# Bf16 matmuls on a filled tile around the first transposes, and five small loads asked for later

## The reference, cut to what matters

```python
def token_mixer(xn, pos_offset, conv_state, ret_state, w_in, conv_w, ret_norm, w_out):
    proj = xn @ w_in                       # 1024 x 3584: xc, gB, gC, q, k, v, g
    ...                                    # short convolution, retention with a state per head
    y = jnp.concatenate([a_out, r_out], axis=-1) @ w_out
    return y, new_conv, new_ret

def decoder_layer(x, ...):
    mix, new_conv, new_ret = token_mixer(rmsnorm(x, norm_mix), ...)
    h = x + mix
    h = h + moe(rmsnorm(h, norm_ffn), w_router, b_router, w_up, b_up, w_down, b_down)
    return h, new_conv, new_ret
...
logits = x @ w_router + b_router           # moe: top 4 of 32 experts
h = xb @ w_up[e] + b_up[e]                 # 1024 x 2048 for each of the 32 experts
return act @ w_down[e] + b_down[e]         # 1024 x 1024 for each
```

## Time and profile before

| | us |
|---|---|
| median of three executions | 1089.33 |
| the profiled execution, its own time | 1087.91 |
| its span, first to last instruction | 1086.0 |
| TensorE's matmul records, busy | 1064.4 |
| VectorE busy | 359.0 |
| memory traffic, mean over the span | 397 GB/s |

### The profile page before, as it was taken

How to read it: one execution, slowest core, us unless ns; L and a number is a source line. 1 busy time by engine, 2 the same in 40 slices (tenths; PEclk the granted TensorE clock), 3 DMA queues, 4 the chain that set the end, 5 groups by cost and what they waited for, 6 DMA issues and landing times.

```text
span 1086.0 us, 13145 instructions
## 1 busy us (share of the span) xinstructions
PE 1064.4 (98%) x5670; PEld 447.3 (41%) x5671; DVE 359.0 (33%) x569; ACT 152.6 (14%) x302; POOL 12.1 (1%) x28
## 2 busy tenths in 40 slices
PE   8999999999999999999999999999999999999997
PEld 6888764333333333333333333333333333333332
DVE  3455534322222222222222222222332222222234
ACT  2121144111111001111111111011111111011113
POOL 1000000000000000000000000000000000000002
PEclk9999999999999999999999999999999999999999
DMA  9875949999999999999999999999999999999994
GB/s 295 308 273 198 405 151 361 418 421 438 427 431 432 428 430 433 431 428 430 433 428 434 430 428 431 432 429 433 433 427 433 433 426 431 426 426 428 428 412 172
DMA packets 40907, 431.47 MB, mean 397 GB/s; under 512 B 4456, under 2 KB 19852, under 8 KB 25104
## 3 DMA queue, kind: packets, MB, share of 16 engines
q1 hardware_dynamic: 40240, 430.41, 94.6%
q10 hardware_dynamic: 608, 0.20, 0.1%
HBM read 427.00 MB, written 3.48 MB: 396 GB/s over the span
## 4 chain that ended last, share of the span: by engine, by line
PE 84%; DMA 15%; DVE 0%; issue 0%; ACT 0%; POOLq 0%; DVEq 0%; POOL 0%; ACTq 0%
PE bank L995 37%; PE bank L1014 16%; DMA ring_all<-in_w_up 14%; PE bank L674 9%; PE bank L1059 6%; PE bank L969 4%; PE bank L1006 2%; PE bank L787 2%; PE bank L977 2%; PE bank L987 1%; PE bank L636 1%; PE bank L1052 1%; PE bank L1071 1%; PE bank L795 1%; PE bank L1097 1%; DMA ident<-in_c_square 0%
## 5 line engine op out<-in xcount | busy, mean ns | idle before, releaser
L995 PE MATMUL bank<-ring_all,work 128*64 128x512 f32 x2048 | 484.6, 600 | 7.4 <-DMA ring_all<-in_w_up 7.4
L995 PEld LDWEIGHTS bank<-ring_all,work 128*64 128x64 f32 x2048 | 134.8, 136 | 257.1 <-issue 247.3
L1014 PE MATMUL bank<-ring_all,work 128*64 128x512 f32 x992 | 225.1, 596 | 1.0 <-DMA ring_all<-in_w_down 1.0
L1810 DVE TENSOR_TENSOR h_tok<-h_tok,bank 128x1024 f32<-128x1024 f32 (+1 forms) x67 | 81.8, 1220 | 236.5 <-PE bank L1059 230.7
L1014 PEld LDWEIGHTS bank<-ring_all,work 128*64 128x64 f32 x992 | 68.5, 137 | 129.8 <-issue 129.4
L674 PE MATMUL bank<-work,ring_all 128*128 128x264 f32 x384 | 86.9, 387 | 0.0
L1780 DVE TENSOR_TENSOR work<-bank,bias_up 128x1024 f32<-128x1024 f32 x32 | 39.2, 1224 | 125.0 <-PE bank L1006 125.0
L674 PEld LDWEIGHTS bank<-work,ring_all 128*128 128x128 f32 x384 | 72.6, 190 | 12.0
L1059 PE MATMUL bank<-work 64*128 64x512 f32 (+1 forms) x268 | 75.2, 638 | 0.0
L1797 DVE TENSOR_TENSOR work<-work 128x512 f32<-128x512 f32 x32 | 22.2, 693 | 108.5 <-ACT work L1398 108.4
L1382 ACT ACTIVATE work<-bank 128x264 f32<-128x264 f32 x32 | 12.5, 390 | 316.3 <-PE bank L987 316.3
(11 more groups left out here) (230 smaller groups left out, 544.8 us busy)
## 6 DMA issues: line engine op xcount, KB each, us to landing
ring_all<-in_w_up SPq DMA_DIRECT2D x48, 4096.0 KB, 33.4
ring_all<-in_w_down SPq DMA_DIRECT2D x24, 4096.0 KB, 34.5
ring_all<-in_w_up SPq DMA_DIRECT2D x30, 2048.0 KB, 38.0
ring_all<-in_w_down SPq DMA_DIRECT2D x13, 2048.0 KB, 40.0
ring_all<-in_w_in SPq DMA_DIRECT2D x13, 1024.0 KB, 5.1
ring_all<-in_w_down SPq DMA_DIRECT2D x6, 1024.0 KB, 21.4
ring_all<-in_w_out SPq DMA_DIRECT2D x4, 1024.0 KB, 10.7
ring_all<-in_w_up SPq DMA_DIRECT2D x4, 1024.0 KB, 5.9
```

The costliest lines, as they stand in the source:

```text
L995: mm = pe.matmul(bank[half * CAP:(half + 1) * CAP, up_bank(n) + b, :].rearrange("q (k p) -> q p k", k=KT), x, src[:, half * FF + b * 512:h ...
L1014: mm = pe.matmul(bank[half * CAP:(half + 1) * CAP, Y, :], av[:, 2 * i + k, :], src[:, k * D + half * 512:k * D + (half + 1) * 512], start= ...
L1810: tt(rows, rows, bank[0:m, b:b + 2, :], ALU.add).then_inc(comb_added, 1)
```

## The change

Two things. First, VectorE fills a bf16 tile `filled` of 128 x 256 with ones as its first instruction. TensorE waits for that and runs 17 matmuls of 256 columns on it before it waits for the identity; one more follows after each half of the two big token tiles (four in all), and two follow after the last transposes. They write to PSUM bank 1, which block 1 of the projection later overwrites, and nobody reads them.

Second, SyncE asks for the state right behind w_in chunk 2 (step j = 2), and for w_rt, b_rt, the two halves of b_up and the copy behind chunk 3 and the first 2 MB of expert weights (step j = 3).

```diff
+            filled = h_tok[:, 2, 512:640].bitcast(BF16)
...
+            fill_ready = sem("fill_ready")
...
-                sp.dma_start(state, state_ret[0].rearrange("b h (x d) e -> (b h x) d e", x=4)).then_inc(state_in, 16)
-                sp.dma_start(w_rt[:], w_router[0].rearrange("(k p) e -> p k e", p=P)).then_inc(misc_in, 16)
-                sp.dma_start(b_rt[:], b_router.partition_broadcast(P)[:, 0, :]).then_inc(misc_in, 16)
-                for half, p0 in enumerate(BU):
-                    sp.dma_start(x_tok[p0:p0 + E, 2, :], b_up[0, :, half * FF:(half + 1) * FF]).then_inc(bu_in, 16)
-                sp.dma_start(conv_sample[0, :, 0, :], state_conv[0, :, 1, :]).then_inc(out_done, 16)
                 for j in range(2, 2 * len(ORDER) + 4):
...
+                    if j == 2:
+                        sp.dma_start(state, state_ret[0]...).then_inc(state_in, 16)
                     if j >= 3:
...
                         if j % 2 and k < FIRST - 1:
                             sp.dma_start(ring_a[:, k, :], chunk_src(stream[k])).then_inc(landed[k], 16)
+                        if j == 3:
+                            sp.dma_start(w_rt[:], ...).then_inc(misc_in, 16)
+                            sp.dma_start(b_rt[:], ...).then_inc(misc_in, 16)
+                            for half, p0 in enumerate(BU):
+                                sp.dma_start(x_tok[p0:p0 + E, 2, :], b_up[...]).then_inc(bu_in, 16)
+                            sp.dma_start(conv_sample[0, :, 0, :], ...).then_inc(out_done, 16)
...
+                def keep_warm(count):
+                    for _ in range(count):
+                        pe.matmul(bank[:, 1, 0:2 * P], filled[:, 0:P], filled, start=True, stop=True)
+
+                pe.wait_ge(fill_ready, 1)
+                keep_warm(17)
                 pe.wait_ge(ident_in, 16)
...
                         mm.then_inc(xt_psum1, 1)
+                        if c < 2:
+                            keep_warm(1)
+                keep_warm(2)
...
+                nc.vector.memset(filled, 1.0).then_inc(fill_ready, 1)
                 nc.vector.memset(small[:, 6:14], 0.0).then_inc(eps_ready, 1)
```

More of the change, by code:

```diff
@@ L497, in _ @@
                         sp.dma_start(wo_slot[i], out_src(i)).then_inc(wo_in[i], 16)
+                    if j == 2:
+                        sp.dma_start(state, state_ret[0].rearrange("b h (x d) e -> (b h x) d e", x=4)).then_inc(state_in, 16)
                     if j >= 3:
@@ L506, in _ @@
                             sp.dma_start(ring_a[:, k, :], chunk_src(stream[k])).then_inc(landed[k], 16)
+                        if j == 3:
+                            sp.dma_start(w_rt[:], w_router[0].rearrange("(k p) e -> p k e", p=P)).then_inc(misc_in, 16)
+                            sp.dma_start(b_rt[:], b_router.partition_broadcast(P)[:, 0, :]).then_inc(misc_in, 16)
+                            for half, p0 in enumerate(BU):
+                                sp.dma_start(x_tok[p0:p0 + E, 2, :], b_up[0, :, half * FF:(half + 1) * FF]).then_inc(bu_in, 16)
+                            sp.dma_start(conv_sample[0, :, 0, :], state_conv[0, :, 1, :]).then_inc(out_done, 16)
                         if j == 17:
```

## The result

The changed kernel takes 1091.05 us (median of 22 executions, 1089.23 to 1095.99) against 1089.05 for the kernel before in the same series (22 executions, 1087.88 to 1091.99). The ratio is 1.0021, with a 95% interval of 1.0012 to 1.0030. It is slower by 2 us, 0.2%, where 1088.2 was forecast and 1090.4 was the top of the range. The 22 times lie in two groups: 14 between 1089.2 and 1091.5 and 8 between 1093.2 and 1096.0.

The account below looks back on a forecast made before the run. TensorE's unbroken chain was taken to bound the start, later balanced against memory at 431 GB/s. Start -2.0 and chunk 4 stall +0.9 gave -1.1 us: 1089.33 to 1088.2 us, range 1086.6 to 1090.4.

Parts of the forecast that it names:

- The start: Fillers before and among the transposes lift the clock sooner; projection and first block gain 1.66 to 2.36 us, taken as 2.0.
- Both cases that were worked out: Two times for the clock's rise at the start: at 7.4 us, or before 5.03 us.
- a rise before 5.03: Clock up before the identity lands: projection starts at 8.65, 1.4 us gained, before adding the first block's 0.96.
- a rise at 7.4: Clock up 6.4 us after TensorE's first work: projection starts at 9.34, 0.7 us gained, before the first block's 0.96.
- 6.4 us after the first work: Reading of the earlier profile: the clock rose at about 11.4 us, TensorE's first work being at 5.03.
- Part two: Five loads asked for later on SyncE, so chunk 2 leaves at once and block 4 keeps the start's gain.
- T: Moment chunk 2 is asked for, right after projection block 1; forecast 16.9 us, or 16.2 after the earlier start.
- the cover: 10 us of slack before TensorE wants the rotated k at about 53, with w_rt's scaling starting near 35.5.
- the gain would be lost at block 4 without part two: With the loads unmoved, chunk 2 still lands near 26.4, so block 4 loses whatever the start gains.
- the +0.9 for chunk 4: Stall at block 8: chunk 4 lands at T + 23.2 but is due at T + 22.25; 0.9 us lost.
- their 2.7 us: Price of the small loads (0.43 MB) in the sum of loads through chunk 4.
- chunk 4 is later than summed: Rival: SyncE held until the expert chunk has passed; stall 2.3 us, net +0.3, 1089.6 us; chance 0.12.

Follow-up runs that it names:

- look_b: The changed kernel unaltered, profiled again as a single execution; 1087.94 us.
- look_a: The changed kernel unaltered, run and profiled once more; 1090.38 us, ratio 1.0013 to the kernel before.
- e7: e4 with the 17 fillers before the identity but without the six between and behind the transposes; 1086.92 us, ratio 0.9976 to the kernel before.
- e8: e4 with no filler at all; 1089.21 us, ratio 0.9995 to the kernel before.
- e2: The changed kernel without fillers, so the moved loads alone; 1093.69 us, ratio 1.0044 to the kernel before.
- e10: e4 with 8 fillers ahead of the identity instead of 17; 1089.91 us, ratio 0.9999 to the kernel before.
- e1: The changed kernel with the fillers alone, the five loads in their old place; 1091.92 us, ratio 1.0019 to the kernel before.
- e3: The changed kernel with router bias, b_up and copy asked for behind chunk 4, w_rt staying at step 3; 1090.97 us, ratio 1.0013 to the kernel before.
- e5: e4 with the state at step 3, behind chunk 3 and the expert chunk; 1090.19 us, ratio 1.0009 to the kernel before.
- e9: The changed kernel with only the state moved, from step 2 to step 4 behind chunk 4; 1089.15 us, ratio 0.9995 to the kernel before.
- e4: The changed kernel with w_rt, bias, b_up and copy behind chunk 2, state behind chunk 4; 1086.45 us, ratio 0.9975 to before; repeated 1087.24, 0.9986.
- e11: e1 with chunk 3 and the expert chunk held back until chunk 2 has landed; 1090.81 us, ratio 1.0014 to the kernel before.
- e6: The changed kernel with the router bias asked for ahead of the router weights w_rt; 1090.59 us, ratio 1.0023 to the kernel before.
- e12: The changed kernel with 28 more fillers, into an unused bank, before block 8; 1091.36 us, ratio 1.0015 to the kernel before.

## Why the prediction was wrong, point by point

**The start was right.** Forecast -2.0 (1.66 to 2.36), measured 2.1 in the profiled execution, 1.6 in look_b, 1.3 in look_a, and 2.3 in median between e7 and e8. Both cases that were worked out occur. In the first profile the clock is up at 3.9 us, 2.7 us behind the first filler, and the projection starts at 8.66 (8.65 for a rise before 5.03). In look_b and look_a it comes up at about 6.7 and 6.9, 5.5 and 5.7 us behind the first filler, and the projection starts at 9.15 and 9.49 (9.34 for a rise at 7.4). The middle between the two was a fair choice, and that one profile hits 2.1 is luck. The first block took 3.80 where 3.56 was summed. Without fillers the clock came 1.4, about 2 and 4.2 us behind the first projection matmul (before, e8, e2), 6.4 to 9.2 us behind the first transpose; e10 kept it low through 5 us of transposes.

That fits the rule of the Trainium skill ("TensorE: Matmul & The Clock Gate", Part 4), that transposes don't count as work that lifts it, better than "6.4 us after the first work". But in e7 and look_a the clock rose while transposes ran, 1.1 and 1.9 us after the last of the 17 had ended, so the rows don't settle it.

**Part two, what was costed at nothing beside it.** Chunk 2 landed 5.7 us after its issue, in time. Chunk 3 was to land by T + 14 and landed at 31.8, T + 15.4: 0.4 us of wait at block 6, not foreseen (in look_a and look_b T + 13.9, no wait). The scaling of w_rt was to start at 35.5 and started at 39.29, since the bias took 13.3 us to land; the cover held, no wait for the rotated k is in the chain.

**That the gain would be lost at block 4 without part two** was right in kind (e1), and too small: the hole was 3.3 us, since chunk 2 landed later than before.

**The step that failed is the +0.9 for chunk 4.** The sum had it land at T + 23.2. It landed at T + 26.4 in the first profile (42.8, with T = 16.46) and at T + 24.2 in look_a and look_b, so the holes are 3.55 and 1.8 us. SyncE's hold was costed at nothing, and the runs do not contradict that: in look_a and look_b chunk 4 is asked for at T + 17.1, as summed (T + 17.2), and e3, which asks for it as soon as its slot is free, lands it at T + 24.9. What is short is the sum of what lies ahead in memory. In look_a and look_b the state lands at T + 10.0, as summed; chunk 3 at T + 13.9 (12.8 by the same prices); the expert chunk at T + 19.4 and 19.6 (17.7); chunk 4 at T + 24.2 (23.2). The prices were added one behind the other, but the router weights, asked for behind the expert chunk, land ahead of it (36.3 against 36.7 in look_a): the loads overlap, and while the small pieces are under way the rate is low (278 GB/s from 32 to 37 us in the change, 433 in e5, where they had landed). The large loads' prices alone were right (e5, 0.3 us off). Take away the state and the hole is 0.7 (e9); put the small loads behind 1 MB only and the state behind chunk 4, and it is nothing (e4). By how much the small loads alone were dearer than their 2.7 us was not measured, and why the first profile's loads were later by 2 us more is open.

Of the rivals, "chunk 4 is later than summed" comes nearest: 1.8 us of stall where it had 2.3, and net +0.5 to +0.8 at block 12 where it had 0.3. Its cause, SyncE held until T + 19.5, is not what happened.

**What wasn't in the prediction at all is the clock behind a hole.** A wait was priced at its length. Behind holes of 3.55 (the change), 3.30 (e1), 3.1 (e2), 3.07 (e11) and 2.5 us (e3) the clock fell, and the blocks that follow took 2.8, 1.7, 1.6, 1.7 and 1.9 us more than before. Behind holes of 1.8 (look_a and look_b), 2.3 (e6) and 2.7 us (e5) it stayed, and they took 0.2 more (14.52 against 14.35). So length alone does not decide (2.5 with a fall, 2.7 without), but every hole of 3 us or more had one.

**Where the median's 2.0 us are.** The net of start and hole is +0.5 to +0.8 us at block 12 in look_a and look_b. The rest goes with the granted clock. The mean granted clock of an execution has its median at 0.996 in both series of the change and at 0.998 in all four series of before. Of the change's 32 executions 11 are at 0.997 or above, of before's 115 it is 99. Among executions of the same clock the change is slower by 0.7 us at 0.997 (1089.98 against 1089.29, means) and by 0.6 at 0.999 (1089.38 against 1088.79). So about a third of the 2.0 us is the late chunk itself, and two thirds go with more time at the low level. e4, with no hole, has 0.999 and 0.9975. In which stretch the middle executions have their falls is not shown, since only profiled ones tell it, and e12, which kept the clock up at block 8, had no better median. look_b, 1087.94, is the fastest of all executions of the change (the next is 1089.08), and 1086.94 is the fastest of before: it is no typical execution.

**What is open.** Why chunk 2 takes 8.3 to 8.7 us in e1 and e11; why the change's hole is 1.8 us in two profiles and 3.55 in a third (chunk 2, the state and chunk 3 already landed 5.7, 10.3 and 8.2 us after their issue there, and 5.1, 9.6 and some 6.7 in look_a and look_b); and what makes the clock fall in the router's stage. In look_a it fell at about 167 us; from 160 to 167 TensorE was busy 6.6 of 7 us, and just as long in look_b, where it did not fall.

## What to carry to other kernels

A wait of TensorE costs more than its length when the clock falls behind it: here holes of 2.5 to 3.6 us cost 1.6 to 2.8 us on top (one of 2.7 did not), so a change that trades a spread slow start for one hole can lose although the sum of waits is even. When loads are moved behind a just-in-time stream, order them by size and need: the small, piecewise ones where the queue is short (behind one chunk the bias held SyncE 1.15 us, behind state, chunk and expert chunk 6.13), and the large one (the 2 MB state) behind the last chunk that is needed soon. The order of e4 keeps the gain of the start: 0.9975 and 0.9986 of the time before in two series.

## What the runs showed of the hardware that I had not expected

- A load of 128-byte pieces (w_rt, 1024 of them) is issued quickly itself (0.43 to 1.2 us), but the next DMA on the same queue is held: 6.13 us in the change, 5.6 to 6.3 in e2, e12 and before, 3.56 without the state ahead (e9), 1.15 and 0.95 behind one chunk (e4, e5). With the order swapped the hold moves to `b_up` (e6, 6.7 us). In e3 chunk 4 came next, 6.2 us later, and its issue took 0.98 us; the bias behind it was held 3.35.
- A too short filler gives nothing: 8 matmuls and a gap of 2 us left the clock low until the first projection block (e10), and block 4 started 1.3 us later than without any in the two profiles; the medians do not tell them apart.
- The same kernel's executions differ by up to 6.8 us on one core, and much of it goes with the mean granted clock: spans of the change at 0.997 to 0.999 lie between 1087.4 and 1089.4, those at 0.992 and 0.993 between 1091.7 and 1094.2. At 0.995 and 0.996 they spread from 1087.7 to 1092.6, so the clock is not all of it.
